# A value panel, the gate of a linear attention and three output splits take earlier places in a float32 block kernel

## The reference

```python
proj = h @ w_in
aq, ak, av, bq, bk, bv, br, blr, cq, ck, cv = jnp.split(proj, split_at, axis=-1)
out_a = rmsnorm(swa_sink_attention(aq, ak, av, ...), swa_out_norm)     # sliding window
gate_pre = blr @ gla_gate_w + gla_gate_b
log_gate = maximum(log_sigmoid(gate_pre) / 16, -1)
o_b = gla_chunked(bq, bk, bv, log_gate)                                # linear attention, 4 heads
out_b = rmsnorm(o_b, gla_norm) * silu(br)
out_c = rmsnorm(stick_breaking_attention(cq, ck, cv), sb_out_norm)     # stick-breaking
x = x + concatenate([out_a, out_b, out_c]) @ w_out
```

## Time and profile before

| | |
|---|---|
| median of 3 runs | 2638.78 us (2638.45 to 2639.59) |
| the profiled execution | 2636.36 us, span 2634.7 us |
| PE busy | 2546.9 us, 97% of the span |
| DVE / ACT / POOL busy | 1766.3 / 1178.8 / 186.4 us |
| chain that ended last | PE 87%, DVE 5%, DMA 3%, ACT 2% |
| HBM traffic | 511.68 MB read, 198 GB/s over the span |

### The profile page before, as it was taken

How to read it: one execution, slowest core, us unless ns; L and a number is a source line. 1 busy time by engine, 2 the same in 40 slices (tenths; PEclk the granted TensorE clock), 3 DMA queues, 4 the chain that set the end, 5 groups by cost and what they waited for, 6 DMA issues and landing times.

```text
span 2634.7 us, 40432 instructions
## 1 busy us (share of the span) xinstructions
PE 2546.9 (97%) x14511; PEld 2218.6 (84%) x14511; DVE 1766.3 (67%) x2225; ACT 1178.8 (45%) x1491; POOL 186.4 (7%) x212
## 2 busy tenths in 40 slices
PE   5999989999999999999899999999999999999999
PEld 4988878888888888878788888887788888888887
DVE  4465465778887876687666666666566656665676
ACT  3444444543443544554233333334455534553453
POOL 2100000000000000032111111110100000000000
PEclk8999999999999999999999999999999999999999
DMA  6754447688777877764666656553556566656555
GB/s 163 250 140 114 127 158 233 223 290 277 234 256 247 264 251 241 265 207 142 192 191 196 197 184 188 184 187 126 152 168 189 178 203 180 191 181 202 181 181 172
DMA packets 277833, 520.74 MB, mean 198 GB/s; under 512 B 30680, under 2 KB 100880, under 8 KB 277072
## 3 DMA queue, kind: packets, MB, share of 16 engines
q1 hardware_dynamic: 251616, 403.66, 48.0%
q0 software_dynamic: 25392, 115.14, 14.5%
q10 hardware_dynamic: 704, 0.29, 0.0%
HBM read 511.68 MB, written 10.49 MB: 198 GB/s over the span
## 4 chain that ended last, share of the span: by engine, by line
PE 87%; DVE 5%; DMA 3%; ACT 2%; issue 1%; ACTq 0%; POOL 0%; DVEq 0%; POOLq 0%; SPq 0%
PE ps L1800 30%; PE ps L1819 21%; PE ps L1822 11%; PE ps L2225 6%; PE ps L2237 5%; PE ps L1792 4%; PE ps L2230 3%; DMA raw<-in_w_in 2%; PE ps L2184 1%; DVE wlo L1104 1%; DVE acc L1379 1%; PE ps L2163 1%; ACT whi L645 1%; PE ps L2054 1%; PE ps L2192 1%
## 5 line engine op out<-in xcount | busy, mean ns | idle before, releaser
L1104 DVE TENSOR_TENSOR wlo<-raw,whi 128x1024 fp32r<-128x1024 f32 (+2 forms) x776 | 939.8, 1222 | 494.3 <-ACT whi L645 473.9
L645 ACT ACTIVATE whi<-raw 128x1024 fp32r<-128x1024 f32 (+2 forms) x776 | 801.1, 1040 | 860.5 <-PE ps L1800 382.8
L1800 PE MATMUL ps<-whi,act 128*128 128x512 f32 (+2 forms) x2608 | 797.3, 387 | 9.4 <-DVE wlo L1104 9.1
L1819 PE MATMUL ps<-act,whi 128*128 128x512 f32 x2400 | 660.4, 396 | 6.6 <-DVE wlo L1104 4.1
L1800 PEld LDWEIGHTS ps<-whi,act 128*128 128x128 f32 x2608 | 485.4, 190 | 104.7 <-issue 9.5
L1800 PE MATMUL ps<-wlo,act 128*128 128x512 f32 (+2 forms) x1304 | 501.3, 384 | 0.0
L1819 PEld LDWEIGHTS ps<-act,whi 128*128 128x128 f32 x2400 | 412.0, 190 | 63.0 <-issue 4.8
L1822 PEld LDWEIGHTS ps<-act,wlo 128*128 128x128 f32 x2400 | 370.9, 190 | 52.3 <-issue 0.2
L1822 PE MATMUL ps<-act,wlo 128*128 128x256 f32 x2400 | 384.5, 282 | 0.0
L1800 PEld LDWEIGHTS ps<-wlo,act 128*128 128x128 f32 x1304 | 247.2, 190 | 45.7
L1379 DVE SCALAR_TENSOR_TENSOR arena<-arena,cond 128x768 f32<-128x768 f32 (+1 forms) x330 | 281.4, 875 | 5.9 <-DMA arena<-in_w_ada 2.9
(11 more groups left out here) (307 smaller groups left out, 2146.3 us busy)
## 6 DMA issues: line engine op xcount, KB each, us to landing
arena<-in_w_ada POOLq DMA_DIRECT2D x128, 768.0 KB, 5.6
raw<-in_ffn_w_up SPq DMA_DIRECT2D x160, 512.0 KB, 4.4
raw<-in_w_mlp_in SPq DMA_DIRECT2D x128, 512.0 KB, 4.7
raw<-in_w_mlp_out SPq DMA_DIRECT2D x128, 512.0 KB, 4.9
raw<-in_na_w_qkv SPq DMA_DIRECT2D x96, 512.0 KB, 4.7
raw<-in_ffn_w_down SPq DMA_DIRECT2D x84, 512.0 KB, 4.3
raw<-in_w_in SPq DMA_DIRECT2D x64, 384.0 KB, 3.6
raw<-in_w_in SPq DMA_DIRECT2D x32, 512.0 KB, 4.5
```

The source lines that it names most:

```text
L645: act.activation(a, b, ACT.Copy).then_inc(hi_done, 1)
L1104: dve.tensor_tensor(a, b, c, ALU.subtract).then_inc(lo_done, 1)
L1800: ins = pe.matmul(o, a, b, start=start and i == 0, stop=last and i == 2, skip_group_check=True)
L1819: pe.matmul(Z[q][:, c, :].rearrange("p (h t) -> p h t", h=2), kn(whi, j)[:, kk, P * c:P * c + P], act2[:, :, k, 0:S], start=k == 0, stop=k ...
```

## The change

It puts panel BV0 ahead of GK, so that BV0 is units 56 to 63 and GK units 64 to 71. The gate (`gla` 0) moves from step 73 to 65 and `gla` 8 from 75 to 68. The two products of `gla` 8 that need the keys become a part of their own, `gla` 9, at step 73, with a wait for GK's copy. `gla` 1 moves from 78 to 76, `norm_a` 2 from 88 to 87, `gate` 0 from 91 to 89. ACT and DVE split units 100 to 102 before `turn` 1 in place of after it.

```diff
 PANELS_IN = [
     ("Q0", 0, 384), ("Q1", 384, 384), ("KV", 768, 512), ("CQ", 3600, 512), ("CK", 4112, 512), ("CV", 4624, 512),
-    ("GQ", 1280, 384), ("GK", 1664, 384), ("BV0", 2048, 400), ("BV1", 2432, 384), ("BR0", 2816, 384),
+    ("GQ", 1280, 384), ("BV0", 2048, 400), ("GK", 1664, 384), ("BV1", 2432, 384), ("BR0", 2816, 384),
...
-        for n, m in ((0, 73), (8, 75), (1, 78), (2, 81), (3, 82), (4, 83), (5, 84), (6, 85), (7, 86)):
+        for n, m in ((0, 65), (8, 68), (9, 73), (1, 76), (2, 81), (3, 82), (4, 83), (5, 84), (6, 85), (7, 86)):
             plan(m, "gla", n)
-        plan(88, "norm_a", 2)
-        plan(91, "gate", 0)
+        plan(87, "norm_a", 2)
+        plan(89, "gate", 0)
         plan(92, "turn", 0)
...
             finish_a("gate", 1)
+            for j in range(4, 7):
+                split(U_OUT, j)
             finish_a("turn", 1)
...
-                for j in range(4, 12):
+                for j in range(4 if n else 7, 12):
                     split(U_OUT, 8 * n + j)
...
-                    own.done(dve.tensor_tensor(g3[0:DK], g3[0:DK], gk[0:DK], ALU.mult))
                     b4 = g1[0:DK].rearrange("p h (c t) -> p (h c) t", t=CH)
                     o4 = g2[0:DK].rearrange("p h (c t) -> p (h c) t", t=CH)
                     last = b4[:, :, CH - 1:CH].to_broadcast([DK, 16, CH])
                     dve.tensor_tensor(o4, last, b4, ALU.subtract).then_inc(gd["d"], 1)
+                if n == 9:
+                    dve.wait_ge(drained[0], 9)
                     dve.wait_ge(gd["ke"], 1)
+                    own.done(dve.tensor_tensor(g3[0:DK], g3[0:DK], gk[0:DK], ALU.mult))
                     dve.tensor_tensor(g2[0:DK], g2[0:DK], gk[0:DK], ALU.mult).then_inc(gd["ki"], 1)
...
             finish_v("gate", 1)
+            for j in range(4, 7):
+                split(U_OUT, j)
             finish_v("turn", 1)
```

## The result

The changed kernel took 2623.33 us (median of 7 runs, 2620.54 to 2628.63), beside 2638.45 for the kernel before in the same comparison (7 runs, 2633.19 to 2646.47). The ratio is 0.9947, interval [0.9934, 0.9959]: 14.0 us less, between 10.8 and 17.4. The three together average 0.9956, 11.7 us. In the comparison that gave 0.9968, one of 29 executions of the kernel before took 3158.05 us, the others 2631.04 to 2643.53; the ratio is made without it.

What follows compares the result with a forecast made beforehand. PE, busy 97% of the span, was taken as the bound, leaving its idle and half-clock time to win. Savings of 3.5 + 1.1 + 6.8 = 11.4 us gave 2625.0 for the profiled execution, 2627.4 for the median; range 2624.8 to 2633.0.

Steps and rivals of the forecast that it cites:

- Part A: Gate and value panel: three GK units cover more of the gate's 12.94 us chain, 3.5 us saved.
- I take 1.7, as 2.5 us lies on the row with 2.49: Behind the gate's 2.5 us idle time PE's clock falls as in one earlier row, 1.7 us lost.
- both cases: Clock behind the gate's idle time: if it holds, 5.2 us saved, chance 0.12; if it falls, 3.5.
- Part B: Normalisation and gate 0 moved earlier: first turning starts after 2.0 us idle, not 3.83; between 0 and 1.9 saved.
- 1.1 us saved: First turning: the turned blocks are written from 363.7, not 364.88; this smaller number was taken as the saving.
- Part C: Three splits ahead of the last turning: PE goes on at 384.98, unit 104 starts 6.0 earlier, 6.8 us saved.
- Load 107: Raw data for unit 107: goes out at about 388.8, lands at 399.5, with 2.3 us of slack.
- ACT would hardly wait for `w_out` data any more: Sign around the last turning: ACT's wait for `w_out` data gone or below 2 us in total.
- transfer rival: Load 107 lands at about 406 behind POOL's 4 MB, 4.2 us late; 5.5 saved, 2633.3 us; chance 0.09.
- A's clock term: Clock loss behind the gate's idle time, put in as 1.7 us where 2.4 was lost before.
- Given back later: Following stage held by something not moving with PE; half or more of the saving lost, 2633 to 2639; chance 0.11.
- the wait of `gla` 9: DVE at step 73 waits for GK's copy and PE runs dry: 2644 us or more; chance 0.04.

Runs made afterwards that it cites:

- one_split: Changed kernel with only unit 100, not 100 to 102, split ahead of the last turning; ratio 0.9958 to the kernel before.
- one_split_spread: one_split with POOL's four loads of 768 KB held back to go out one by one; one execution of 2627.77 us.
- only_a: Kernel before with only BV0 ahead of GK and the new places of `gla` 0, 8, 9 and 1; ratio 0.9983.
- all_again: Changed kernel run a second time, nothing altered; ratio 0.9968 to the kernel before, profiled execution 2620.79 us.
- changed first: First run of the changed kernel, against the kernel before; ratio 0.9947, median 2623.33 us, profiled execution 2625.64 us.
- all_third: Changed kernel run a third time, nothing altered, on the chip of the three others; ratio 0.9952 to the kernel before.
- only_b: Kernel before with only `norm_a` 2 moved to step 87 and `gate` 0 to step 89; ratio 1.0000.
- gate_step: Changed kernel with ACT's and DVE's half of the gate one step later than PE's, behind the split of unit 69; ratio 0.9935 to the kernel before.
- only_c: Kernel before with only the early splits of units 100 to 102 ahead of the last turning; ratio 0.9983.
- gate_turn: gate_step with PE's first turning a step later than ACT's and DVE's, `gate` 0 at step 90; ratio 0.9931 to the kernel before.
- gate_turn_spread: gate_turn with POOL's four loads held back to go out one by one; ratio 0.9932 to the kernel before.
- before_spread: Kernel before with POOL's first four modulation loads held until PE has used units 102, 104, 106 and 108; one execution of 2633.14 us.

## Why the prediction was right and wrong

**Part A.** The 12.9 us of the gate's chain and its cover by three GK units held to 0.1 us: idle 2.39 to 2.40 in all six executions with this order. The wait of 0.74 went, and units 72 and 77 came in time. The step that failed is "I take 1.7, as 2.5 us lies on the row with 2.49". The clock held in four of the six executions with this idle time (the first and third of the changed kernel, one_split and one_split_spread) and fell in two, only_a and all_again. One row of one execution was read as a rule. The price itself was right: where the clock fell it cost 1.4 to 1.7 us. With the clock held A is worth 5.8 us, not 3.5, and with the clock low 4.1 to 4.5. So both cases lie 0.6 or more above their forecast, 5.2 and 3.5. The idle time accounts for 0.1 of this; where the rest comes from stays open. Cheaper BV0 units beside stick-breaking are not the source, as of three such units one took 3.38 us and the other two 7.03 together, 10.4 in all for 3 x 3.44 = 10.3.

**Part B.** The start of the transposes moved by 2.3 us and their end by 1.8, forecast 1.8 and 1.1. The term "1.1 us saved" was too small by 0.7. The working also left out the clock behind it: it spoke of an idle time of 2.0 us ahead of the turning, gave PE's wait inside the turning no length, and priced neither in clock. The pair 1.57 and 1.55 cost 1.6 us more in four of seven executions that had it (changed first, all_third, one_split, one_split_spread; not in all_again, only_b, gate_step). On average over the seven B brought about 0.9. That this is near the 1.1 is luck: a larger saving, less a loss of clock that was not in the sum.

**Part C.** Forecast 6.8, by the marks 6.0 to 7.9 (28.3 to 29.0 against 35.0 to 36.2). PE went on at once, and the turned blocks were not delayed. Load 107 was said to go out about 4.3 us behind the start of the last transposes and to land in time with 2.3 us of slack; it landed 15.6 us behind that start, at 397.0 in the row of ACT (forecast 15.0), and was split 2 us ahead of PE. That ACT would hardly wait for `w_out` data any more was wrong (12.7 us for 16.0 in before), and it was a poor sign: by the prediction's own times ACT had to wait for load 107 until 399.5, and with slack behind it the wait costs nothing. The transfer rival did not come, but it was nearer than its 0.09. The working stopped at load 107, and the tight one is 108: it went out at 387.4, took 14.1 us, and its split ended at 403.9, just as PE took the unit up at 403.95. The same unit came 0.58 late in all_again, 0.26 in all_third and 0.23 in only_c, which is what C varies by, and one_split shows the rival at its full size.

**Sum and range.** For the profiled execution the forecast was 2625.0 and the measurement 2625.64. That is luck in good part, since errors cancelled: by the marks A brought 4.2 there (5.8, less 1.7 for the longer low clock at 222 us) for 3.5, B with the stretch behind it 0.2 for 1.1, C 6.7 for 6.8, the start lost 1.3 and the end gave 0.8. For the median the range was too narrow at its lower end: it held the clock of A and B's bounds but not the scatter of the executions, which is 8 us within seven runs of the changed kernel and 13 within seven of before, while the three runs of before that the prediction started from lay within 1.1 us. The failed steps together: A's clock term, 1.7 us put in and nothing measured in four executions of six; what else A was short, 0.6; B's end, 0.7; and a scatter left at nothing. With the clock held in A and B and the measured sizes, 5.8 + 1.8 + 6.7 = 14.3 us, the median would be 2624.5: just below the range, and still 1.2 above the measured 2623.3. No part was found for these 1.2 us; they are small beside what separates the three comparisons, 14.0, 8.4 and 12.7 us. At its other end the range stops at 2633.0, just short of the transfer rival's own 2633.3. "Given back later" and the wait of `gla` 9 did not come; the stretch to the end took as long as before.

## What to carry to other kernels

When a chain on other engines is fixed in length, ask how many units of the bound engine are ready ahead of it, and let the helpers prepare one more while they wait anyway: moving ACT's and DVE's half one step behind PE's took away the last 2.4 us, for 0.5 of a new one. When a stall is removed, follow the loads that the old stall had given time to: two early splits that by themselves spared PE a wait of 0.8 us were worth over 4, because they sent loads out ahead of a crowd. And compare such changes by marks in the trace before medians: ahead of 420 us, stretches without a change agree to 0.1 us where the clock is the same, while the intervals of the ratios here reach 2.4 to 4.7 us to either side. Then read the clock at every mark, and not at the changed place alone: all_again and all_third both took 96.3 us in A, one with the clock low behind the gate and the other at 222 us.

## What the runs showed of the hardware

The clock behind an idle time of 1.6 to 2.5 us is a draw: the same program with the same idle time kept it in one execution and lost it in another. After the 2.4 us behind the gate it held four times and fell twice. Two idle times of 1.6 us, 2 us of work apart, brought it down in four executions of seven. Behind the 2.48 to 2.55 us at 222 us it fell in thirteen executions of fourteen and held in all_again; in nine of the thirteen this cost about 1.7 us, in the other four (the first of the changed kernel, only_a, gate_turn, gate_turn_spread) about 3.4. Outside this band there was no draw between 222 and 425 us: behind the idle times of 3.5 to 4.6 us (twelve, in before, only_a, only_b, only_c and before_spread) there was a window of 2 us with the granted clock at 0.50 to 0.55 every time, and behind those of 0.8 us and less, where it was full ahead of them, it never fell. What decides inside the band was not tried. The Trainium skill says in TensorE: Matmul & The Clock Gate, section The HAM clock gate (the "warmup" mystery), that the moment at which the clock rises under steady work differs from run to run. The traces agree: at 222 us it came back after a loss of 1.7 us in some executions and of 3.4 in others.

The clock was also below full while PE stood nowhere. In one_split, in the middle of the MLP, PE was busy for 50.00 of 50 us and the granted clock was 0.93:

```profile
700.00:750.00 50.00, 50.00 (x273) 43.74 (x272) 36.58 (x35) 25.21 (x26) 2.84 (x4) 0.93 0.71 232
```

That is 3.5 us lost in one stretch, and its part from the next turning to 1122.8 us took 710.2 us for 705.3 in before. It is no peculiarity of this execution: each of the fourteen has one to four windows of 25 us between 425 and 1300 us in which PE was busy for 25.00 and the clock was 0.93 or lower, before the one from 550 to 575 for example. What brings the clock down there was not tried. From 425 us on the clock cost 15 to 24 us in all, most in one_split and one_split_spread (24 and 23), which have the longest last stretches, 2220.0 and 2217.1. Among the other twelve the order does not follow the clock (before_spread lost 15 us and took 2213.0, gate_turn_spread 21 and 2212.7), so it explains a part of the scatter that hid A, B and C from the medians, and not all.
